# Order of wide and narrow matmuls inside a unit of the two-half blocks

## The chip, the cores and the metric

The kernel runs on one core of one Trainium2 chip. The metric is the device time of one execution in microseconds (us). The notes below use the names of the profile: PE is the matrix engine (TensorE), PEld its weight loads, DVE the vector engine, ACT the scalar engine, POOL GpSimd, and SP the engine that issues the weight stream's DMAs.

## The reference

Two transformer-like blocks for one sequence of 256 tokens of width 2048, all in float32. What matters here is that nearly all of the time goes into products of 256 tokens with large weight matrices:

```
def reference(x, ...):
    x = first_block(x, ...)       # h @ w_in, sliding-window attention, short conv, @ w_out, @ w_ple_gate
    return second_block(x, ...)   # @ w_in_2, recurrence, selected attention, @ w_o, then peer()

def peer(x, wq, keys1, keys2, u, v):      # 16384 experts, top 16 per head
    q = (xf @ wq) ...
    ...
    z = jnp.einsum('cd,ced->ce', xc, u[ec])
    act = jax.nn.gelu(z, approximate=False) * gc
    return jnp.einsum('ce,ced->cd', act, v[ec])
```

The kernel computes the expert layer densely: all of u and v (128 blocks of 128 experts each) is streamed and multiplied, and a table of gates picks the experts.

## The kernel before, in words

**Precision by halves.** Every float32 operand is split into a high part and a low part, and a product is made of three: high weights by high activations, high weights by low activations, and low weights by high activations.

**Units.** All weights arrive as one stream of 902 units of 128 x 1024 float32 (512 KB), in four slots of `raw`. For each unit ACT makes the high weights (`split_hi`, L495: `w_hi <- raw`, raises `hi_ready`) and DVE the low ones (`split_lo`, L504: `w_lo <- raw - w_hi`, raises `lo_ready`). PE multiplies, and its last matmul of a unit raises `unit_done`; ACT and DVE wait for `unit_done` of the unit four back before they write the same slot again. SP loads the next unit into a slot as soon as `lo_ready` shows that its `raw` was used. Every wait is written out by hand; there is no scheduler.

**Blocks of two-half form.** `halves_out` makes one block of 128 output columns from two units (`u` is 0 or 1), 8 slices of 128 rows of weights in each. For a slice, one *wide* matmul multiplies the high weights by high and low activations side by side (512 columns, L561, into all of a PSUM bank: low sums land in the upper half), and one *narrow* matmul multiplies the low weights by the high activations (256 columns, L568, added to the lower half). Behind the block ACT copies the upper half out (L574) and DVE adds the lower half to it (L579). 240 blocks, so 480 units, have this form: the stages conv, rnn, heads, wqu, u_decode, u_gates and u_late. Each stage is a loop on PE that calls `halves_out` and stands beside loops on ACT, DVE and POOL of the same stage.

**Two options.** `between` is called in a block's second unit only; in u_gates it is `two_tokens` (L2658), two small matmuls that build the table of gates from `hot` and `weighted`, which DVE writes. `paced` is set for one block, the first of wqu: there each wide matmul first waits for its slice of the activations (`act_lo_ready`, DVE L1959).

**The other forms.** In the last stage, `v` (L2693 to L2695), and in `tokens_out` (L601 to L603) the weights are the 512-column moving operand; all their matmuls are wide. These do not pass through `halves_out`.

Of the kernel before, what the change touches and what calls it, by code (L numbers as in the profile page):

```python
# [35 lines left out]
P = 128  # L36
S = 256
TT = S // P
D = 2048
KT = D // P  # L40
# [99 lines left out]
def build(nc, stream, x, p_t, rows, consts, params, rg_w, ukv, keys_t, out):  # L140
    ctx = ExitStack()
    with ctx:
        def sb(name, shape, dt=F32):
            return ctx.enter_context(nc.sbuf_tensor(name, shape, dt))

        def sem(name):
            return ctx.enter_context(nc.semaphore(name))
# [3 lines left out]
        w_hi = sb("w_hi", [P, SLOTS, UNIT], F32R)  # L151
        w_lo = sb("w_lo", [P, SLOTS, UNIT], F32R)
        act2 = sb("act2", [P, KT, 2, S], F32R)
        act_hi = act2[:, :, 0, :]
# [187 lines left out]
        lo_ready = sem("lo_ready")  # L342
# [29 lines left out]
        act_lo_ready = sem("act_lo_ready")  # L372
# [112 lines left out]
        def unit_slot(odd, u):  # L485
            return 2 * odd + u
# [65 lines left out]
        def halves_out(pe, pair, odd, bank, units=(0, 1), between=None, paced=None):  # L552

            for u in units:
                s = unit_slot(odd, u)
                pe.wait_ge(hi_ready, 2 * pair + u + 1)
                for kk in range(8):
                    k = 8 * u + kk
                    if paced:
                        pe.wait_ge(act_lo_ready, paced + k + 1)  # L560
                    pe.matmul(bank[:, :], w_hi[:, s, kk * P:(kk + 1) * P],  # L561
                              act2[:, k, :, :].rearrange("p a n -> p (a n)"), start=(k == 0), stop=False)
                if u and between:
                    between()
                pe.wait_ge(lo_ready, 2 * pair + u + 1)
                for kk in range(8):
                    k = 8 * u + kk
                    mm = pe.matmul(bank[:, 0:S], w_lo[:, s, kk * P:(kk + 1) * P], act_hi[:, k, :], start=False,  # L568
                                   stop=(k == KT - 1))
                mm.then_inc(unit_done, 1)  # L570

        def low_half(act, dest, bank):
# [1662 lines left out]
        def _(pe):  # L2235
# [89 lines left out]
            def conv_pair(j, n):  # L2325
                wait_summed(pe, block_of("conv", j, 4, n - 4))
                halves_out(pe, pair_of("conv", j, 4, n), odd_of("conv", n), banks[n])
# [141 lines left out]
            def rnn_inputs(j):  # L2469
                wait_summed(pe, block_of("rnn", j, 2, 0 - 2))  # L2470
                halves_out(pe, pair_of("rnn", j, 2, 0), odd_of("rnn", 0), banks[0])

            def rnn_queries(j):
                wait_summed(pe, block_of("rnn", j, 2, 1 - 2))
                halves_out(pe, pair_of("rnn", j, 2, 1), odd_of("rnn", 1), banks[1])
# [368 lines left out]
```

## Time and profile before

| what | value |
|---|---|
| median of 3 runs | 2696.33 us (2696.3 to 2696.57) |
| profiled execution, whole | 2696.89 us |
| its span, first to last instruction | 2695.2 us |
| PE busy | 2669.4 us (99% of the span) |
| granted TensorE clock, mean | 0.999 of full speed |
| matmuls in the span | 14299, of them 3840 wide and 3840 narrow in `halves_out` |

The span is what the trace shows; the profiled execution's own time is 1.69 us more, which lies around the span. Busy time of PE counts a matmul from its start until its modelled end, and consecutive matmuls overlap, so the rows that tell the pace of PE are the distances from one start to the next.

### The profile page before, as it was taken

The page shows a single profiled execution, that of the slowest core. Times are in us where ns is not written, and L with a number is a line of the kernel's source. Part 1 is how long each engine was busy: PE and PEld are TensorE (multiplying, and loading weights), DVE is VectorE, ACT ScalarE, POOL GpSimd, SP SyncE. Part 2 cuts the span into 40 slices and gives each one's busy share as a digit, 9 for nine tenths or more (in the row PEclk, how much of TensorE's full clock was granted, in tenths as well). Part 3 has the DMA queues.
Part 4 walks back from the last instruction along what each step waited for, and adds up shares of the span by engine and source line. Part 5 has one row for each costly group of instructions (what it writes and reads, how often), then busy time and mean ns, then how long its engine had stood idle before and what let it go on. Part 6 is the DMA issues. An engine that isn't in the chain of part 4 may idle for free.

```text
span 2695.2 us, 47112 instructions
## 1 busy us (share of the span) xinstructions
PE 2669.4 (99%) x14299; PEld 2298.4 (85%) x14299; DVE 1835.3 (68%) x2985; ACT 1369.4 (51%) x2066; POOL 371.4 (14%) x296
## 2 busy tenths in 40 slices
PE   8999999999999999999999999999999999999998
PEld 6888888898888998888888888888888888888887
DVE  6666665668987677489996777775565555555555
ACT  6454445555665444455455555554444444444444
POOL 0010000001011211011105555551000000000000
PEclk9999999999999999999999999999999999999999
DMA  7566555564554554655567777777976666666564
GB/s 257 189 216 213 181 199 177 177 219 159 172 176 156 167 168 157 195 201 186 195 201 212 202 202 203 201 204 218 305 240 217 217 217 219 212 220 216 200 241 156
DMA packets 204475, 543.26 MB, mean 202 GB/s; under 512 B 37504, under 2 KB 82816, under 8 KB 203392
## 3 DMA queue, kind: packets, MB, share of 16 engines
q1 hardware_dynamic: 148112, 486.74, 54.9%
q10 hardware_dynamic: 35568, 47.33, 5.0%
q0 software_dynamic: 20736, 8.46, 2.7%
q8 instruction: 30, 0.49, 0.1%
q14 instruction: 29, 0.24, 0.0%
HBM read 515.12 MB, written 27.33 MB: 201 GB/s over the span
## 4 chain that ended last, share of the span: by engine, by line
PE 94%; DVE 3%; ACT 1%; issue 1%; DMA 0%; SPq 0%; DVEq 0%; POOL 0%; ACTq 0%; POOLq 0%
PE bank L561 32%; PE bank L568 16%; PE bank L2693 8%; PE bank L2694 8%; PE bank L2695 8%; PE bank L601 4%; PE bank L603 4%; PE bank L602 4%; PE bank L2488 1%; DVE w_lo L504 1%; PE bank L527 1%; PE bank L528 1%; PE bank L529 1%; PE bank L2658 1%; PE bank L2465 0%
## 5 line engine op out<-in xcount | busy, mean ns | idle before, releaser
L504 DVE TENSOR_TENSOR w_lo<-raw,w_hi 128x1024 fp32r<-128x1024 f32 x902 | 1097.9, 1226 | 725.9 <-ACT w_hi L495 719.4
L495 ACT ACTIVATE w_hi<-raw 128x1024 fp32r<-128x1024 f32 x902 | 950.8, 1059 | 946.5 <-PE bank L568 363.1
L561 PE MATMUL bank<-act,w_hi 128*128 128x512 f32 x3840 | 975.2, 396 | 2.6 <-DVE cst L579 1.0
L561 PEld LDWEIGHTS bank<-act,w_hi 128*128 128x128 f32 x3840 | 692.0, 189 | 133.8 <-issue 6.4
L568 PEld LDWEIGHTS bank<-act,w_lo 128*128 128x128 f32 x3840 | 519.7, 190 | 33.1
L568 PE MATMUL bank<-act,w_lo 128*128 128x256 f32 x3840 | 535.6, 282 | 0.0
L2693 PE MATMUL bank<-w_hi,expert_act 128*128 128x512 f32 x1008 | 392.3, 389 | 0.1
L2694 PE MATMUL bank<-w_lo,expert_act 128*128 128x512 f32 x1008 | 392.2, 389 | 0.0
L2695 PE MATMUL bank<-w_hi,expert_act 128*128 128x512 f32 x1008 | 392.1, 389 | 0.0
L742 POOL DMA_INDIRECT g_kept<-slot_t x128 | 239.7, 1872 | 253.8 <-issue 170.4
L2693 PEld LDWEIGHTS bank<-w_hi,expert_act 128*128 128x128 f32 x1008 | 189.3, 188 | 39.6 <-DVE cst L579 0.5
L2695 PEld LDWEIGHTS bank<-w_hi,expert_act 128*128 128x128 f32 x1008 | 189.3, 188 | 39.3
L2694 PEld LDWEIGHTS bank<-w_lo,expert_act 128*128 128x128 f32 x1008 | 189.3, 188 | 39.1
L601 PE MATMUL bank<-w_hi,act 128*128 128x512 f32 x320 | 125.8, 393 | 2.0 <-DVE act L1401 1.1
L603 PE MATMUL bank<-w_hi,act 128*128 128x512 f32 x320 | 124.7, 390 | 0.0
L602 PE MATMUL bank<-w_lo,act 128*128 128x512 f32 x320 | 124.6, 389 | 0.0
L748 POOL TENSOR_TENSOR big<-big 128x1024 f32<-128x1024 f32 x2 | 5.8, 2878 | 839.4 <-DVE big L2196 839.4
L601 PEld LDWEIGHTS bank<-w_hi,act 128*128 128x128 f32 x320 | 60.1, 188 | 16.2 <-DVE w_lo L504 1.3
L603 PEld LDWEIGHTS bank<-w_hi,act 128*128 128x128 f32 x320 | 60.1, 188 | 12.6
L602 PEld LDWEIGHTS bank<-w_lo,act 128*128 128x128 f32 x320 | 60.1, 188 | 12.1
L729 POOL TENSOR_TENSOR big<-big 128x256 f32<-128x256 f32 x32 | 33.1, 1034 | 248.3 <-ACT big L1138 248.3
L2107 DVE SCALAR_TENSOR_TENSOR weighted<-cst,slot_t 128x256 fp32r<-128x256 f32 x128 | 61.3, 479 | 0.0
(344 smaller groups left out, 2498.4 us busy)
## 6 DMA issues: line engine op xcount, KB each, us to landing
raw<-in_stream SPq DMA_DIRECT2D x902, 512.0 KB
z_kept<-cst ACTq DMA_DIRECT2D x112, 128.0 KB, 2.4
cst<-z_kept ACTq DMA_DIRECT2D x112, 128.0 KB, 3.9
g_kept<-zeros POOLq DMA_DIRECT2D x16, 512.0 KB
big<-in_ukv ACTq DMA_DIRECT2D x16, 512.0 KB, 4.6
big<-g_kept SPq DMA_DIRECT2D x16, 512.0 KB, 5.6
big<-in_rows ACTq DMA_DIRECT2D x3, 1024.0 KB, 5.8
big<-in_x SPq DMA_DIRECT2D x2, 1024.0 KB, 10.2
```

The source lines that it names most:

```text
L495: act.activation(w_hi[:, s, :], raw[:, s, :], ACT.Copy).then_inc(hi_ready, 1)
L504: dve.tensor_tensor(w_lo[:, s, :], raw[:, s, :], w_hi[:, s, :].bitcast(F32), ALU.subtract).then_inc(lo_ready, 1)
L561: pe.matmul(bank[:, :], w_hi[:, s, kk * P:(kk + 1) * P], act2[:, k, :, :].rearrange("p a n -> p (a n)"), start=(k == 0), stop=False)
L568: mm = pe.matmul(bank[:, 0:S], w_lo[:, s, kk * P:(kk + 1) * P], act_hi[:, k, :], start=False, stop=(k == KT - 1))
L601: pe.matmul(outs[t], a_hi, hi, start=(k == 0), stop=False)
L602: pe.matmul(outs[t], a_hi, lo, start=False, stop=False)
L603: mm = pe.matmul(outs[t], a_lo, hi, start=False, stop=(k == KT - 1))
L742: pool.indirect_dma_start(g_kept, bass.IndirectOffsetOnAxis(ap=SLOT_INDEX[:, i:i + 1], axis=0), SLOT_GATE[:, i:i + 1], None, compute_op=AL ...
L2107: dve.scalar_tensor_tensor(out=weighted[:, tile, :, :], in0=iota.unsqueeze(1).broadcast_to([P, 2, P]), scalar=first_index[:, bass.ds(tok, 1)],
L2693: pe.matmul(o, a_hi, hi, start=first, stop=False, skip_group_check=True)
L2694: pe.matmul(o, a_hi, lo, start=False, stop=False, skip_group_check=True)
L2695: mm = pe.matmul(o, a_lo, hi, start=False, stop=False, skip_group_check=True)
```

## The change

In each unit the eight wide and eight narrow matmuls are issued in another order. Before: all eight wide ones, then `between` (second unit only), then the wait for the low weights, then all eight narrow ones. Now: four wide ones, then `between`, then the wait for the low weights, then the other four wide ones alternating with the first four narrow ones, then the last four narrow ones. The operands of each matmul, the bank it adds to, the number of instructions and the last matmul of the unit, which raises `unit_done`, are the same.

```diff
             for u in units:
                 s = unit_slot(odd, u)
                 pe.wait_ge(hi_ready, 2 * pair + u + 1)
-                for kk in range(8):
-                    k = 8 * u + kk
-                    if paced:
-                        pe.wait_ge(act_lo_ready, paced + k + 1)
-                    pe.matmul(bank[:, :], w_hi[:, s, kk * P:(kk + 1) * P],
-                              act2[:, k, :, :].rearrange("p a n -> p (a n)"), start=(k == 0), stop=False)
-                if u and between:
-                    between()
-                pe.wait_ge(lo_ready, 2 * pair + u + 1)
-                for kk in range(8):
-                    k = 8 * u + kk
-                    mm = pe.matmul(bank[:, 0:S], w_lo[:, s, kk * P:(kk + 1) * P], act_hi[:, k, :], start=False,
-                                   stop=(k == KT - 1))
+                for kk in range(12):
+                    if kk == 4:
+                        if u and between:
+                            between()
+                        pe.wait_ge(lo_ready, 2 * pair + u + 1)
+                    if kk < 8:
+                        k = 8 * u + kk
+                        if paced:
+                            pe.wait_ge(act_lo_ready, paced + k + 1)
+                        pe.matmul(bank[:, :], w_hi[:, s, kk * P:(kk + 1) * P],
+                                  act2[:, k, :, :].rearrange("p a n -> p (a n)"), start=(k == 0), stop=False)
+                    if kk >= 4:
+                        k = 8 * u + kk - 4
+                        mm = pe.matmul(bank[:, 0:S], w_lo[:, s, (kk - 4) * P:(kk - 3) * P], act_hi[:, k, :],
+                                       start=False, stop=(k == KT - 1))
                 mm.then_inc(unit_done, 1)
```

On PE, in the loop of stage u_late, one unit stood like this before (a row is an instruction or a run of equal ones, with the semaphores it waits for; L561 is the wide matmul, L568 the narrow one):

```order
L561 MATMUL bank<-act,w_hi 128x512 [waits hi_ready]
L561 MATMUL bank<-act,w_hi 128x512 x7
L568 MATMUL bank<-act,w_lo 128x256 [waits lo_ready]
L568 MATMUL bank<-act,w_lo 128x256 x7
```

The same unit now, where the wide matmul is L566 and the narrow one L570:

```order
L566 MATMUL bank<-act,w_hi 128x512 [waits hi_ready]
L566 MATMUL bank<-act,w_hi 128x512 x3
L566 MATMUL bank<-act,w_hi 128x512 [waits lo_ready]
L570 MATMUL bank<-act,w_lo 128x256
L566 MATMUL bank<-act,w_hi 128x512
L570 MATMUL bank<-act,w_lo 128x256
L566 MATMUL bank<-act,w_hi 128x512
L570 MATMUL bank<-act,w_lo 128x256
L566 MATMUL bank<-act,w_hi 128x512
L570 MATMUL bank<-act,w_lo 128x256 x5
```

Three narrow matmuls now stand between two wide ones, and the wait for the low weights has moved ahead of the fifth wide one.

On PE, in the second unit of a u_gates block, where the two token matmuls (L2658 before, L2660 now) stand, before:

```order
L561 MATMUL bank<-act,w_hi 128x512 [waits hi_ready]
L561 MATMUL bank<-act,w_hi 128x512 x7
L2655 REGISTER_ALU
L2656 ISA [waits gate_kept0]
L2658 MATMUL bank<-weighted,hot 128x256 [waits hot1]
L2658 MATMUL bank<-weighted,hot 128x256
L568 MATMUL bank<-act,w_lo 128x256 [waits lo_ready]
L568 MATMUL bank<-act,w_lo 128x256 x7
```

and now:

```order
L566 MATMUL bank<-act,w_hi 128x512 x3
L2657 REGISTER_ALU
L2658 ISA [waits gate_kept0]
L2660 MATMUL bank<-weighted,hot 128x256 [waits hot1]
L2660 MATMUL bank<-weighted,hot 128x256
L566 MATMUL bank<-act,w_hi 128x512 [waits lo_ready]
L570 MATMUL bank<-act,w_lo 128x256
L566 MATMUL bank<-act,w_hi 128x512
```

The token matmuls and their waits for `gate_kept` and `hot1` have moved ahead of four wide matmuls as well.

## Rows read from the trace of the kernel before

**Rows 1.** The page: busy time by engine, then the chain that ended last by engine and line.

```profile
PE 2669.4 (99%) x14299; PEld 2298.4 (85%) x14299; DVE 1835.3 (68%) x2985; ACT 1369.4 (51%) x2066; POOL 371.4 (14%) x296
...
PE 94%; DVE 3%; ACT 1%; issue 1%; DMA 0%; SPq 0%; DVEq 0%; POOL 0%; ACTq 0%; POOLq 0%
PE bank L561 32%; PE bank L568 16%; PE bank L2693 8%; PE bank L2694 8%; PE bank L2695 8%; PE bank L601 4%; PE bank L603 4%; PE bank L602 4%; PE bank L2488 1%; DVE w_lo L504 1%; PE bank L527 1%; PE bank L528 1%; PE bank L529 1%; PE bank L2658 1%; PE bank L2465 0%
```

**Rows 2.** The page's costliest groups: xcount | busy us, mean ns | idle before, by releaser.

```profile
L561 PE MATMUL bank<-act,w_hi 128*128 128x512 f32 x3840 | 975.2, 396 | 2.6 <-DVE cst L579 1.0
...
L568 PE MATMUL bank<-act,w_lo 128*128 128x256 f32 x3840 | 535.6, 282 | 0.0
```

**Rows 3.** The chain in order of time, stage u_late: start us, length us, what.

```profile
1934.88 1.84 PE bank L561 x8
1936.72 0.95 PE bank L568 x8
1937.67 1.84 PE bank L561 x8
```

**Rows 4.** The chain in order of time, stage u_gates, around two token matmuls.

```profile
1501.97 0.23 PE bank L2658 x2
1502.20 0.96 PE bank L568 x8
```

**Rows 5.** Timeline of PE, one unit of u_late and the next's first: start us, us.

```profile
1937.51 0.40 PE L561 MATMUL bank<-act,w_hi 128*128 128x512 f32 x1
...
1937.74 0.40 PE L561 MATMUL bank<-act,w_hi 128*128 128x512 f32 x1
...
1937.98 0.39 PE L561 MATMUL bank<-act,w_hi 128*128 128x512 f32 x1
...
1938.67 0.39 PE L561 MATMUL bank<-act,w_hi 128*128 128x512 f32 x1
...
1939.35 0.28 PE L568 MATMUL bank<-act,w_lo 128*128 128x256 f32 x1
...
1939.46 0.40 PE L568 MATMUL bank<-act,w_lo 128*128 128x256 f32 x2
...
1939.58 0.40 PE L568 MATMUL bank<-act,w_lo 128*128 128x256 f32 x2
...
1940.30 0.40 PE L561 MATMUL bank<-act,w_hi 128*128 128x512 f32 x1
```

**Rows 6.** Line L2693 of stage v: count, ns min/median/max, first and last start us.

```profile
L2693 PE MATMUL bank<-w_hi,expert_act x1008: 389/389/500, 1990.6 to 2675.7; 128*128 128x512 f32 x168
```

**Rows 7.** Timeline, stage rnn, around a late low half: start us, us, what.

```profile
622.25 3.05 DVE L504 TENSOR_TENSOR w_lo<-raw,w_hi 128x1024 fp32r<-128x1024 f32 x1
...
626.31 2.00 PE L561 MATMUL bank<-act,w_hi 128*128 128x512 f32 x8
...
628.15 1.12 PE L568 MATMUL bank<-act,w_lo 128*128 128x256 f32 x8
```

**Rows 8.** Timeline, stage u_gates, ahead of two token matmuls.

```profile
1806.17 0.48 DVE L2107 SCALAR_TENSOR_TENSOR weighted<-cst,slot_t 128x256 fp32r<-128x256 f32 x1
...
1808.78 2.00 PE L561 MATMUL bank<-act,w_hi 128*128 128x512 f32 x8
...
1810.62 0.40 PE L2658 MATMUL bank<-weighted,hot 128*128 128x256 f32 x2
```

**Rows 9.** Timeline of the paced block's second unit, PE and DVE.

```profile
1161.64 3.22 DVE L1959 SCALAR_TENSOR_TENSOR act<-bank,par,act 128x256 fp32r<-128x256 f32 x8
...
1162.26 3.15 PE L561 MATMUL bank<-act,w_hi 128*128 128x512 f32 x8 [0.17 <-DVE act L1959]
1165.24 1.00 PE L568 MATMUL bank<-act,w_lo 128*128 128x256 f32 x7
```

## The prediction

> **What bounds the kernel now.** I read the page first: PE is busy for 99% of the span, and the chain of work that ended last runs over PE for 94%, the wide and the narrow matmuls of `halves_out` alone for 32% and 16% [rows 1]. So the kernel is as long as PE's row of matmuls, and only two things can change it here: the distance from one matmul's start to the next, and waits of PE. Next the costliest groups: 3840 wide and 3840 narrow matmuls, that is 480 units of eight and eight, and idle time before them of 2.6 us and 0.0 us in all [rows 2]. No narrow matmul has waited for its low weights, so no wait is there to be removed. What is left is the pace.
>
> **The pace, read off the starts.** In order of time the chain shows a unit as 1.84 us of wide matmuls and 0.95 us of narrow ones, 2.79 us in all [rows 3]. The timeline of one unit tells more [rows 5]. The first five wide matmuls take 1938.67 - 1937.51 = 1.16 us, 0.232 each. The last three take 1939.35 - 1938.67 = 0.68 us, 0.227 each. That is the pace of stage v as well, where all matmuls are wide: (2675.7 - 1990.6) us over 1007 x 3 starts is 0.2268 us [rows 6]. Of the narrow ones the first takes 0.11 us, the second 0.12, and the other six 1940.30 - 1939.58 = 0.72 us, 0.120 each. The hundredths of a timeline are too coarse for the first, so I take it from the chain: eight narrow ones take 0.95 us behind a wide matmul [rows 3], and 0.96 us, eight times 0.120, behind the two token matmuls, which are narrow too and take 0.23 us together where two at 0.120 would take 0.24 [rows 4]. The first narrow matmul behind a wide one thus takes about 0.113 us, half of 0.227, and those behind another narrow one 0.119 to 0.120.
>
> So a switch has two sides. Going from wide to narrow, one matmul comes 0.007 us early. Going from narrow to wide, the wide ones are 0.005 us late on the mean, over five of them. A unit has one switch of each kind before and four of each now.
>
> **The change part by part.**
>
> Instructions: none is added or removed, and none of other engines moves; PE issues no DMA, and `unit_done` still stands on the last narrow matmul, so that ACT's and DVE's next units and SP's loads behind them follow a unit's end as before.
>
> Narrow matmuls: the first four now each stand behind a wide one. The second to fourth of them lose 0.119, 0.120 and 0.120 for 0.113: 0.020 us for a unit. The fifth then takes the second's place (0.119 for 0.120). That is 480 x 0.020 = 9.6 us, if each behaves as the first does now.
>
> Wide matmuls: the sixth to eighth now each stand behind a narrow one, where they were in the settled 0.227. The trace of before has no wide matmul behind a single narrow one. The bound from below is 0.227, no loss. The nearest row is the unit's first wide one, behind eight narrow ones: 0.23 us, and the second takes 0.24 [rows 5]. With the mean of 0.232 of the first five the three lose 3 x 0.005 = 0.015 us; with 0.007, what the narrow one had gained, 0.021; with the 0.236 that 0.24 may round from, 3 x 0.009 = 0.027. I take 0.020, equal to the gain: the nearest row by kind is the first wide one, and a 0.007 that a narrow one gets by having its weights ready, and that the wide one behind it then pays because its own weights had only the short narrow one to load under, is one and the same time. The sum of both terms is 0 for a unit.
>
> This is also where a rule speaks against the change. The Trainium skill (TensorE: Matmul & The Clock Gate, Step-by-step: what each phase is for) says that only the weight loads are pulled ahead, the next tile's weights loading while this tile's matmul runs, and that the matmuls keep their order. By it each narrow matmul has one load to cover, whatever stands behind it, and the eight of a unit cost the same in any order: a change of 0. No row of before shows a second load ahead, nor rules it out.
>
> The wait for the low weights moves up by four wide matmuls, 4 x 0.23 = 0.92 us. Queued behind it are those four and all narrow ones, and for them wait ACT and DVE (the slot) and the block's copy. The closest call that I found over the 480 units is in stage rnn, where a low half took 3.05 us and was done at 625.30; the narrow matmuls that need it began at 628.15, and the new place is 626.31 + 0.93 = 627.24 [rows 7]. So 1.9 us of cover remain where it is least, and the cost is 0. Were the cover gone, a unit would pay up to 0.92 us.
>
> The token matmuls move up as far. Their `weighted` was written by 1806.65 for a start at 1810.62 [rows 8]; of 3.97 us, 3.05 remain. Cost 0. They are a pair of narrow ones between wide ones now, a further switch in 64 units (two blocks in each of 32 turns): +0.007 for the wide one behind and as much less for the narrow one that they stood ahead of.
>
> The paced block: its second unit's wide matmuls come at the pace of DVE, 0.40 us each, 2.98 us from the first to the first narrow one [rows 9]. Three narrow ones of 0.12 now fit into three gaps of about 0.16: 0.36 us less, once.
>
> Sum: 0 - 0.4 us. The profiled execution took 2696.89 us (span 2695.2 and 1.69 around it), so 2696.5; the median of the runs stands 0.56 below the profiled one, which makes **2696.0 us**.
>
> **The rivals.**
>
> *Narrow ones hidden (faster).* The 0.120 of a narrow matmul behind a narrow one is a shortage (of weight loading or of issue, the row does not say which) that a wide one beside it makes good, and the wide one pays nothing. For it: the first narrow one does gain. Against it: eight wide ones in a row buy only about one narrow one its gain, and the next wide ones are late. Time: 480 x 0.020 = 9.6 us and the 0.4, so 2686.3. The Trainium skill (TensorE: Matmul & The Clock Gate, Wait — 56ns, not 53.3ns?) has a rule of this kind: without hardware decode the sequencer spends about 62 ns on a matmul; an estimate of two instructions by it gives 0.124 us for load and matmul, where the rows show 0.120, and by it the alternation would gain the 9.6 us.
>
> *Each switch is paid for (slower).* A wide matmul behind a narrow one starts the settling of five wide ones anew, and the narrow ones between do not get their 0.007 since the wide one ahead is not settled either. Place: the sixth to eighth wide matmul of each unit. Price: 0.005 to 0.009 each, 0.015 to 0.027 a unit, and 0.007 more if the first narrow one loses its gain too: 7 to 16 us, so 2703 to 2712, in the middle 2706. It decides from the point at which a pair of wide and narrow takes more than 0.347 (0.227 + 0.120) on the mean. For it: before, a unit is about 0.02 us longer than eight pairs of 0.347 (2.774 against 2.79), so a switch is not free in sum.
>
> *A wait takes its place.* The low weights are late at the new place. Against it the 1.9 us of cover; six units late by the whole 0.92 us would make 0.2%. I give it 2 in 100.
>
> **How the numbers follow.** About 0.2%, 5.4 us, or 0.011 us a unit, is what a measurement of this kernel can tell from no change. No change, 2696.0: 0.52. Narrow ones hidden: 0.22, nearly all beyond the limit. Switches paid for, the late low weights included: 0.26. The range reaches over the faster case's 2686.3 and takes the slower one's lower and middle part, to 2708; what lies above needs the highest price for all three wide ones. The likeliest case's own range is 2691 to 2701. Faster by over 0.2%: 0.22; within: 0.52; slower: 0.26.
>
> **What would show it.** In the changed trace a pair of wide and narrow in the alternation takes 0.347 us (0.340: hidden; 0.350 or more: paid for). Narrow starts in it come 0.113 apart from the next wide, and the wide ones there take 0.234. A unit of u_late stays at 2.79 us. Idle time before the wide and narrow groups stays under 3 us in all, and the wide ones of the paced block keep DVE's pace with narrow ones between them. The forecast is wrong if units differ by more than 0.011 us, or if PE waits for DVE's low half anywhere in `halves_out`.

## The result, and the profile after

The changed kernel takes 2701.26 us (median of 22 runs) where the kernel before takes 2696.39 us (22 runs): a ratio of 1.0018, 95% interval 1.0012 to 1.0024. It is slower by 4.9 us, less than the 0.2% that the prediction named as its limit, but clear of the noise of so many runs. (One of the 22 runs before took 4458.5 us; without it the median is 2696.35.) The forecast was 2696.0 with no change as the likeliest; the time lies in the whole range, on the slower side, and 0.3 us above the 2701 at which the range of no change ended.

The page of the changed kernel, to be held against [rows 1, 2]: busy time by engine, the chain that ended last, the two groups of matmuls, which now have the lines L566 (wide) and L570 (narrow).

```profile
span 2699.4 us, 47114 instructions
...
PE 2674.1 (99%) x14299; PEld 2296.5 (85%) x14299; DVE 1835.0 (68%) x2985; ACT 1370.1 (51%) x2066; POOL 370.9 (14%) x296
...
PE 93%; DVE 4%; ACT 1%; issue 1%; DMA 0%; SPq 0%; POOL 0%; DVEq 0%; ACTq 0%; POOLq 0%
...
L566 PE MATMUL bank<-act,w_hi 128*128 128x512 f32 x3840 | 1162.9, 398 | 2.4 <-DVE big L1508 0.8
...
L570 PE MATMUL bank<-act,w_lo 128*128 128x256 f32 x3840 | 766.2, 281 | 0.0
```

PE is as full as before, and nothing stands idle ahead of the wide and narrow matmuls: 2.4 and 0.0 us. The busy sums of the groups (1162.9 and 766.2 us, before 975.2 and 535.6) tell nothing of cost: consecutive records overlap, and when the two lines alternate the overlap is counted in both. The span is 4.2 us longer. None of it is idle time ahead of these two groups, so it lies in the pace of PE or in waits of other matmuls; below, both turn up.

The timeline of PE, one unit of u_late, to be held against [rows 5]:

```profile
1941.30 1.32 PE L566 MATMUL bank<-act,w_hi 128*128 128x512 f32 x5
1942.46 0.28 PE L570 MATMUL bank<-act,w_lo 128*128 128x256 f32 x1
1942.58 0.40 PE L566 MATMUL bank<-act,w_hi 128*128 128x512 f32 x1
1942.81 0.28 PE L570 MATMUL bank<-act,w_lo 128*128 128x256 f32 x1
1942.93 0.40 PE L566 MATMUL bank<-act,w_hi 128*128 128x512 f32 x1
1943.17 0.28 PE L570 MATMUL bank<-act,w_lo 128*128 128x256 f32 x1
1943.29 0.40 PE L566 MATMUL bank<-act,w_hi 128*128 128x512 f32 x1
1943.52 0.76 PE L570 MATMUL bank<-act,w_lo 128*128 128x256 f32 x5
1944.12 1.32 PE L566 MATMUL bank<-act,w_hi 128*128 128x512 f32 x5
```

The unit takes 1944.12 - 1941.30 = 2.82 us, before 2.79. The three wide matmuls that stand behind a narrow one take 0.23, 0.24 and 0.23 us. The trace keeps starts to the nanosecond; the distances from each start to the next, as medians over the units of u_late, are (W wide, n narrow):

```
before  W 233 236 228 232 231 227 227 227   n 113 119 120 120 120 120 120 120            unit 2793 ns
after   W 233 236 228 233 231  n 113 W 233 n 117 W 241 n 120 W 236 n 113   n 119 120 120 120   unit 2813 ns
```

The eight wide ones take 30 ns more (6, 14 and 9 in the three that moved), the narrow ones 10 ns less. 20 ns in 32 units is 0.64 us, and that is what u_late has grown by, from 89.27 to 89.91 us between its first wide and its last narrow start. By the same measure conv grew by 0.40 us, rnn by 0.96, heads by 0.09, wqu by 0.77, u_decode by 0.11 and u_gates by 1.57. That is 4.5 us in all; the rest of the kernel took some 0.3 us less.

Of the 1.57 us in u_gates a part is a wait. The waits of PE have one row that the kernel before did not have, and the timeline shows its place, the first token pair of the stage:

```profile
PE bank L2660 <- DVE weighted L2109: 0.8, 1, 0.8
```

```profile
1443.52 1.09 PE L566 MATMUL bank<-act,w_hi 128*128 128x512 f32 x4
1445.40 0.50 PE L2660 MATMUL bank<-weighted,hot 128*128 128x256 f32 x2 [0.78 <-DVE weighted L2109]
```

The block's first unit began at 1440.71 and the next block at 1447.62 us, 6.91 us; before it was 5.98 (1438.75 to 1444.73). So 0.93 us are lost there, once.

In the other 63 token units the alternation runs at another pace. The timeline of one in u_gates:

```profile
1502.88 1.09 PE L566 MATMUL bank<-act,w_hi 128*128 128x512 f32 x4
1503.81 0.40 PE L2660 MATMUL bank<-weighted,hot 128*128 128x256 f32 x2
1504.04 0.39 PE L566 MATMUL bank<-act,w_hi 128*128 128x512 f32 x1
1504.27 0.28 PE L570 MATMUL bank<-act,w_lo 128*128 128x256 f32 x1
1504.39 0.39 PE L566 MATMUL bank<-act,w_hi 128*128 128x512 f32 x1
...
1505.08 0.39 PE L566 MATMUL bank<-act,w_hi 128*128 128x512 f32 x1
1505.31 0.75 PE L570 MATMUL bank<-act,w_lo 128*128 128x256 f32 x5
```

From 1504.04 to 1505.08 three pairs of a wide and a narrow matmul take 1.04 us, where the three pairs of the u_late unit from 1942.46 to 1943.52 take 1.06. The same instructions on the same shapes take 0.347 us a pair here and 0.353 there. Over the whole kernel the three pairs ran at the fast pace in 120 units (63 in u_gates, 26 in conv, 22 in heads, 5 in u_decode, 4 in rnn) and at the slow pace in the other 360, but for one that keeps DVE's pace (the second unit of the paced block). From its first to its last start a fast unit takes 7 ns less than the same unit before, 0.87 us in all. A slow one takes 16 ns more on the mean, 5.6 us in all (the unit that waits for the tokens and the two units of the paced block are left out of this).

### The profile page after: what moved, and what is told of

The parts are those of the page before. It is cut to its first block, busy times and chain, and to the rows that moved or that the text cites. A ratio compares the mean times of both kernels' runs of the same rounds, so it can differ in the third digit from the quotient of the medians.

```text
span 2699.4 us, 47114 instructions
## 1 busy us (share of the span) xinstructions
PE 2674.1 (99%) x14299; PEld 2296.5 (85%) x14299; DVE 1835.0 (68%) x2985; ACT 1370.1 (51%) x2066; POOL 370.9 (14%) x296
## 4 chain that ended last, share of the span: by engine, by line
PE 93%; DVE 4%; ACT 1%; issue 1%; DMA 0%; SPq 0%; POOL 0%; DVEq 0%; ACTq 0%; POOLq 0%
PE bank L566 31%; PE bank L570 16%; PE bank L2695 8%; PE bank L2696 8%; PE bank L2697 8%; PE bank L603 4%; PE bank L605 4%; PE bank L604 4%; DVE w_lo L504 1%; PE bank L2490 1%; PE bank L527 1%; PE bank L528 1%; PE bank L529 1%; PE bank L2660 1%; ACT w_hi L495 1%
## 5 line engine op out<-in xcount | busy, mean ns | idle before, releaser
L566 PE MATMUL bank<-act,w_hi 128*128 128x512 f32 x3840 | 1162.9, 398 | 2.4 <-DVE big L1508 0.8
L566 PEld LDWEIGHTS bank<-act,w_hi 128*128 128x128 f32 x3840 | 691.5, 189 | 133.2 <-issue 6.3
L570 PE MATMUL bank<-act,w_lo 128*128 128x256 f32 x3840 | 766.2, 281 | 0.0
L570 PEld LDWEIGHTS bank<-act,w_lo 128*128 128x128 f32 x3840 | 622.7, 189 | 39.9
```

Source lines behind the costliest of these rows:

```text
L566: pe.matmul(bank[:, :], w_hi[:, s, kk * P:(kk + 1) * P], act2[:, k, :, :].rearrange("p a n -> p (a n)"), start=(k == 0), stop=False)
L570: mm = pe.matmul(bank[:, 0:S], w_lo[:, s, (kk - 4) * P:(kk - 3) * P], act_hi[:, k, :], start=False, stop=(k == KT - 1))
```

## The experiments

The order in a unit is given by a string: W is the next wide matmul, n the next narrow one. Experiments 1, 2, 6, 7 and 10 keep the instructions of a unit and change their order alone; 3 and 4 widen the narrow matmuls, 5 gives the two units of a block different orders, 8 uses another bank and 9 adds matmuls. Each cut shows only the lines that matter, and `...` stands for what is left out. The names ORDER, BETWEEN_AT (the place of the token matmuls) and WAIT_AT (the place of the wait for the low weights) stand for values that each kernel has written in.

```diff
-                for kk in range(12):
+                wide = narrow = 0
+                for at, form in enumerate(ORDER):
+                    if at == BETWEEN_AT and u and between:
+                        between()
+                    if at == WAIT_AT:
+                        pe.wait_ge(lo_ready, 2 * pair + u + 1)
...
```

**1. The early wait and tokens without the alternation.** "Alternation" is the stretch in which wide and narrow matmuls take turns.

```diff
+ORDER = "WWWWWWWWnnnnnnnn"; BETWEEN_AT = WAIT_AT = 4
```

> The order of the matmuls of before (eight wide, eight narrow); only the wait for the low weights and the two token matmuls stand behind the fourth wide one, as in the change. Theory A (the alternation itself costs, in the pace of the matmuls): no difference from before beyond 2 us, a unit of u_late stays at 2.79 us, no idle time ahead of a wide or narrow matmul beyond 3 us in all. Rival B (the early wait or the early token matmuls cost): 4 to 5 us slower than before, 2701.

Measured: 2698.0 us, ratio 1.0006 (0.9997 to 1.0016). The units of u_late take 2.793 us as before: the wait itself costs nothing. In u_gates alone the stage grew by 1.76 us (462.33 to 464.09): the first token pair waits here too (6.91 us for that block, 0.93 more than before), and the others are a switch more in the run of wide matmuls. The chain in order of time shows it: four wide ones ahead of the pair, four behind, and those take 0.93 us, where four settled ones take 0.91.

```profile
1506.38 0.93 PE bank L567 x4
1507.31 0.23 PE bank L2663 x2
1507.54 0.93 PE bank L567 x4
1508.47 0.96 PE bank L572 x8
```

So neither theory was right as put: outside u_gates no stage grew by more than 0.05 us, so there it is the alternation that costs, as theory A said, but in u_gates the early place of the tokens costs too. The time as a whole cannot be told from before.

**2. Full alternation.**

```diff
+ORDER = "WnWnWnWnWnWnWnWn"; BETWEEN_AT = 4; WAIT_AT = 1
```

> All eight pairs alternate (wide, narrow, wide, ...), with the low weights waited for behind the first wide one. Theory A1 (each switch from narrow to wide is paid for, 4.9 us for three further ones): seven further ones cost 7/3 as much, 11 us slower, 2708, a pair takes 0.350 us on the mean. Rival A2 (the pace depends on how the matmuls stand to each other when the alternation begins; in a steady alternation they fall into the pairs of 0.230 and 0.117 that the token units of the change show): a unit of u_late takes 8 x 0.347 = 2.78 us instead of 2.79, some 8 us faster than before, 2688.

Measured: 2705.1 us, ratio 1.0032 (1.0019 to 1.0045): 8.6 us slower, between the two forecasts and with the sign of A1. A2's time was a miss, but the trace bears out its view that the pace depends on how the alternation is entered: steady stretches run at one of two paces. Timeline of PE, first in u_decode, then in u_late:

```profile
1365.93 0.39 PE L567 MATMUL bank<-act,w_hi 128*128 128x512 f32 x1
1366.16 0.28 PE L572 MATMUL bank<-act,w_lo 128*128 128x256 f32 x1
1366.28 0.39 PE L567 MATMUL bank<-act,w_hi 128*128 128x512 f32 x1
...
1368.01 0.39 PE L567 MATMUL bank<-act,w_hi 128*128 128x512 f32 x1
```

```profile
1949.97 0.40 PE L567 MATMUL bank<-act,w_hi 128*128 128x512 f32 x1
1950.21 0.28 PE L572 MATMUL bank<-act,w_lo 128*128 128x256 f32 x1
1950.33 0.40 PE L567 MATMUL bank<-act,w_hi 128*128 128x512 f32 x1
...
1952.09 0.40 PE L567 MATMUL bank<-act,w_hi 128*128 128x512 f32 x1
```

Six pairs take 2.08 us in the first (0.347 each) and 2.12 us in the second (0.353). To the nanosecond the first repeats 230 117, elsewhere 231 112 233 117, both with a mean of 0.347 us a pair; the second repeats every three pairs 233 117 241 120 236 113, which is what the units of the change run through. Within u_decode the pace turns from the first to the second ahead of the stage's last turn, where three small transposes of PE stand between the units:

```
unit of u_decode   starts at us   distances of its 16 starts, each to the next, ns
28                 1424.99        230 117 230 116 230 117 230 117 230 116 230 117 230 117 230 118
29                 1428.01        315 117 233 118 241 120 236 113 232 118 241 120 236 113 232 118
30                 1430.92        241 120 236 113 232 118 241 120 236 113 232 118 241 120 236 113
```

All of u_gates and u_late then stays at the second (u_gates is 6.4 us longer than before, u_late 1.1); conv, heads and wqu, which PE's other work cuts into short stretches, show both, and are no slower than before (201.39, 254.21 and 186.99 us against 201.45, 254.25 and 187.67). In rnn, cut up as well, 62 of 64 units ran at the second, and it is 1.6 us longer.

**3 and 4. Narrow matmuls of 384 columns,** in the order of before and in that of the change. The low weights then also multiply a part of the low activations, a small product more.

```diff
-                    mm = pe.matmul(bank[:, 0:S], w_lo[...], act_hi[:, k, :], ...)
+                    mm = pe.matmul(bank[:, 0:384], w_lo[...], act2[:, k, :, :].rearrange("p a n -> p (a n)")[:, 0:384], ...)
```

> The order of before, but the narrow matmuls are 384 columns wide (the low weights also multiply the low activations of half the tokens, which adds a small product to the upper sums). Theory L (a 256-column matmul is too short to cover the next weight load, and a wide one behind it pays): at 384 columns there is no shortage, narrow ones come at 384/512 of 0.2267, 0.170 us, all wide ones at 0.227, a unit of u_late takes 3.17 us. Rival F (a switch of form or a fixed cost of each matmul, whatever the load): 0.173 us for a narrow one (0.120 plus 128 columns at 0.107 per 256) and the first five wide ones still at 0.232: 3.22 us. Time some 480 x 0.38 = 180 us above before, 2878.

> The order of the change with narrow matmuls of 384 columns, to be compared with the kernel of 384 columns in the order of before. Theory L (short cover of the weight load): no difference between the two, within 2 us. Rival F (each switch of form costs): again 4 to 5 us slower than that kernel.

Measured: 2913.4 and 2913.8 us, the same within their spread; the forecast of 2878 was 35 us too low. The chain of the first, with wide matmuls at 1.85 us for eight and narrow ones at 1.42, 0.177 each:

```profile
1944.85 1.39 PE bank L572 x8
1946.24 1.85 PE bank L567 x8
1948.09 1.42 PE bank L572 x8
```

A unit of u_late takes 3.267 us in the order of before and 3.260 alternating. Both are above theory L's 3.17 and rival F's 3.22. The narrow ones reach 0.173, rival F's number, in the last two of eight, and the wide ones behind them do not settle at all within eight (229 233 236 224 231 236 228 233 ns). So theory L, that a narrow matmul of 256 columns is too short to cover the next weight load, falls by experiment 3: at 384 columns the wide ones behind are even less settled. Its forecast for experiment 4, no difference, came true, but not for its reason: an alternating pair takes 0.407 to 0.411 us in u_late, where a settled wide and a settled narrow one would take 0.400, so the alternation is off the settled pace here too, and the runs of eight that it replaces are about as far off. Rival F falls in its second half: the switches of the change add nothing to the time there.

**5. Mirrored units.** The second unit of a block runs its narrow matmuls first.

```diff
+                order = "nnnnnnnnWWWWWWWW" if u and not paced else "WWWWWWWWnnnnnnnn"
```

> The first unit of a block as before (eight wide, eight narrow); the second the other way round (eight narrow, then eight wide), so that the narrow matmuls of a block stand in one run of sixteen and the wide ones of two blocks too: half the switches of before. The paced block keeps the old order. Every theory by which a switch from narrow to wide costs about 0.020 us more than a switch back gives (0.027 over five wide ones against 0.007) says 240 x 0.020 = 4.9 us faster: 2691.6, two units of u_late take 5.566 us instead of 5.587. If what counts is only the state in which a stretch is entered and the wide ones behind sixteen narrow ones settle more slowly or not at all, it is no faster: 2696 or above.

Measured: 2695.0 us, ratio 0.9997 (0.9988 to 1.0006): no difference that can be told. Two units of u_late take 2.766 + 2.801 = 5.567 us, where 5.566 was expected, and the chain shows the runs of sixteen:

```profile
1940.37 1.91 PE bank L574 x16
1942.28 3.65 PE bank L568 x16
1945.93 1.91 PE bank L574 x16
```

But u_gates, from its first start to u_late's, took 461.75 us where it took 462.45 before: it gained 0.7 us instead of 80 x 0.020 = 1.6. The forecast of 2691.6 was a miss: the span fell by 2.1 us, not 4.9. Sums for a stage made from one unit's pace held in u_late and not in u_gates.

**6. Two narrow ones ahead of the alternation.**

```diff
+ORDER = "WWWWnnWnWnWnWnnn"; BETWEEN_AT = WAIT_AT = 4
```

> Order in a unit: four wide, two narrow, then the other four wide alternating with four narrow, then two narrow: one switch more than the change has. Theory P (an alternation runs in one of two repeating patterns, 0.347 us or 0.353 us for a pair, by the state in which it is entered; entered behind two narrow ones, as the token units of the change show, it runs in the fast one): the wide ones in it take 0.230, the narrow ones 0.117, a unit of u_late 2.78 to 2.79 us, 4 to 8 us faster than before, 2688 to 2692. Rival A1 (every further switch from narrow to wide is paid for alike, 1.6 us each over the kernel): four further ones, 6.5 us slower than before, 2703.

Measured: 2703.1 us, ratio 1.0025 (1.0015 to 1.0035). My forecast for theory P was a miss: in u_late the wide and narrow ones run through 233 118 240 120 236 114 232 118, the slow pattern, and a unit takes 2.820 us. In heads, where other matmuls stand between the units, the same order runs at the fast pace in 31 of 64 units. Two narrow matmuls ahead do not by themselves choose the pattern. The time is rival A1's 2703, and so is the unit: with one switch more than the change it takes 7 ns more.

**7. The tokens late, in the change.**

```diff
+ORDER = "WWWWWnWnWnWnnnnn"; BETWEEN_AT = 11; WAIT_AT = 4
```

> The change, but the two token matmuls stand behind the eighth wide matmul again instead of behind the fourth. Theory P (the token pair makes its unit's alternation start in the fast pattern): without it these 64 units run in the slow pattern like the others, and the change is 1 to 3 us slower than it was: 2702.5 to 2704, u_gates from its first wide to its last narrow matmul 465 to 467 us where the change took 463.9. Rival B (the early token pair is itself what costs there, 1.8 us in u_gates in the kernel that only moved it): faster than the change by that, 2699.5, u_gates 462.2.

Measured: 2702.6 us, ratio 1.0023 (1.0013 to 1.0032); u_gates 465.37 us. That is theory P: the first token pair no longer waits (5.87 us for that block), yet u_gates is 1.47 us longer than in the change, because the token units now run 113 233 117 241 120 236 as the others do. Only the trace can tell this: by the runs as a whole, the interval overlaps with that of the change (1.0012 to 1.0024). In u_gates the two parts of the change do not add up: before 462.33 us, with the early tokens alone 464.09 (experiment 1), with the alternation alone 465.37 (here), with both 463.90.

**8. The narrow matmuls in a bank of their own,** in u_late alone, in the order of the change.

```diff
+                        mm = pe.matmul((bank if other is None else other)[:, 0:S], w_lo[...], act_hi[:, k, :], ...)
...
+                    halves_out(pe, ..., banks[2 + n], other=banks[6 + n])
```

> The order of the change; in stage u_late alone the narrow matmuls add up in a PSUM bank of their own, which nothing reads (that stage's low-weight terms are left out of the sums). Theory Q (what costs is that a half-bank and a whole-bank matmul follow each other in one bank): in u_late the pattern 0.233, 0.117, 0.241, 0.120, 0.236, 0.113 is gone and a unit takes 2.79 us or less. Theory P (it is the state in which the alternation is entered, on the operands' side): the same pattern as in the change, 2.813 us a unit.

Measured, a single run: 2701.1 us; u_late 89.91 us, a unit 2.813, the same pattern. Theory Q falls. The order in u_gates is that of the change here, and again 63 of its 64 token units run at the fast pace.

**9. One matmul inserted ahead of each turn of u_late,** in the full alternation.

```diff
-            with pe.Fori(0, LATE // 2) as i:
+            for i in range(LATE // 2):
+                pe.matmul(banks[7][:, 0:64 * (i + 1)], act_hi[:, 0, 0:P],
+                          act2[:, 0, :, :].rearrange("p a n -> p (a n)")[:, 0:64 * (i + 1)], start=True, stop=True)
```

> All eight pairs alternate as in the full alternation; the eight turns of stage u_late are written out, and ahead of each stands one further matmul of 64, 128, ... 512 columns into a bank that nothing reads. Theory P (the state at the entry decides between 0.347 and 0.353 us a pair): u_late, which ran at 0.353 throughout, now shows both paces, one or the other for whole turns, changing where a matmul was inserted. Rival T (the stage decides: its operands, its transfers): 0.353 in all eight turns, but for the first few pairs behind the inserted matmul.

Measured, a single run: 2705.0 us. The timeline of PE around the second inserted matmul (L2677, 128 columns): six pairs ahead of it, from 1916.08 to 1918.20, and six behind it, from 1919.38 to 1921.46.

```profile
1916.08 0.40 PE L567 MATMUL bank<-act,w_hi 128*128 128x512 f32 x1
...
1918.20 0.40 PE L567 MATMUL bank<-act,w_hi 128*128 128x512 f32 x1
...
1918.91 0.22 PE L2677 MATMUL bank<-act 128*128 128x128 f32 x1
...
1919.38 0.40 PE L567 MATMUL bank<-act,w_hi 128*128 128x512 f32 x1
...
1921.46 0.40 PE L567 MATMUL bank<-act,w_hi 128*128 128x512 f32 x1
```

2.12 us before, 2.08 us behind. Turn by turn u_late ran slow (64 columns), fast (128), slow (192), slow (256), and fast in the last four (320 to 512), each pace held to the end of its turn. That is theory P's forecast; rival T falls, since all eight turns belong to the same stage.

The same trace shows that the order of the instructions is not the whole of the entry. Up to u_late this kernel gives PE the instructions of experiment 2 in the same order. Yet u_decode runs at the fast pace in 28 of 32 units there and in 2 of 32 here. They ran on different chips; whether that, or a wait on the way to u_decode, made the difference is not known. So a stage's pace can differ from one execution to another, and there is one trace of each kernel.

**10. One pair alone.**

```diff
+ORDER = "WWWWWWWnWnnnnnnn"; BETWEEN_AT = WAIT_AT = 7
```

> Seven wide matmuls, one narrow, the eighth wide, seven narrow: one further switch of each kind, where the change has three. Theory A1 (each switch costs alike): a third of the change's 0.020 us, 2.800 us for a unit of u_late, 1.6 us slower in all. Theory P (the slow pattern's first pair is no longer than 0.347, its second and third are): 2.797 us or less for a unit, 0 to 1.9 us slower in all.

Measured, a single run: 2698.9 us; a unit of u_late takes 2.800 us, A1's number and not P's. Its wide one behind the first narrow one takes 232 and the narrow one next 118, about as P has it, but the narrow ones that follow do not settle at 120 either (121 120 124 117 118 121), and the next unit begins with 237 235. What P leaves out is that a run of narrow matmuls can be entered unsettled as well.

## Why the prediction was wrong, point by point

**The bound and the cover: right.** PE's pace is what the time follows. The wait for the low weights at its new place cost nothing (0.0 us idle ahead of L570; experiment 1's unit of u_late). The paced block's two units took 6.99 us from the first wide one's start to the next block's, where they took 7.35 before: 0.35 us less, with 0.36 forecast.

**The narrow and the wide terms: mis-sized, both to the slow side.** The step that failed is "the sum of both terms is 0 for a unit". I let every narrow matmul behind a wide one gain 0.007 us as the first does in [rows 5], 0.020 in all, and let the wide ones lose as much. In u_late the narrow ones gained 0.010 and the wide ones lost 0.030, more than my upper bound of 0.027 from the second wide one of a unit. 0.020 us of the sum is left, in the units that run so. The picture of one and the same time passed from a narrow to a wide matmul was wrong: the pair does not keep a sum of 0.347 us. The prediction's own signs say the same: a unit of u_late differs by more than 0.011 us, and its pairs take more than 0.350. The time fell inside the range because the range took in part of the slower rival, not because the sum held.

**What stands in its place.** A steady alternation ran at one of two paces, 0.347 or 0.353 us for a pair, in repeating patterns, and how it is entered decides which. Experiment 9 shows it most directly: its eight turns differ only in the columns of the matmul inserted ahead of each, and whole turns run at one pace or the other. Experiment 2 shows the pace turning within one stage, behind three transposes, and 7 shows that the token pair is what put the token units of the change on the faster pace. In u_late the change enters the slow one, three pairs of it in a unit: 3 x 0.0067 = 0.020 us, which is the whole growth of the unit. Over the kernel 359 of 480 units enter the slow one, and in heads and conv, where a third or more enter the fast one, the stage grows less. What it is in PE that the entry sets is not shown.

**The token matmuls: wrong.** I read the cover of a pair late in the stage, 3.97 us [rows 8], and costed the move at 0. The first pair has no such cover: it waits 0.78 us, and its block is 0.93 us longer. Even before, that pair started 0.28 us behind the wide matmul ahead of it, where the settled distance is 0.227. The row to read was that of the stage's first turn. Beyond the wait, the pair between the wide ones cost some 0.8 us over the other 63 units in experiment 1, and with the alternation it brought the faster pace instead; the prediction had put this switch at nothing in sum.

**The rivals.** Hidden narrow ones fell: eight switches of each kind instead of one cost 8.6 us rather than gain (experiment 2). The rule of the Trainium skill beside that rival (TensorE: Matmul & The Clock Gate, Wait — 56ns, not 53.3ns?) would, by the estimate made from it, have given a gain as well, and the trace does not show one. The other rule of the Trainium skill (TensorE: Matmul & The Clock Gate, Step-by-step: what each phase is for), that the weights of the next tile load while this tile's matmul runs, agrees with the traces: in u_late each weight load starts 1 to 5 ns behind the start of the matmul ahead of its own, before the change and after it. So no second load ran ahead, which the prediction had left open. The conclusion that I drew from that rule, the same cost in any order, does not hold: the order and what ran before make a difference. The slower rival named the right place, the sixth to eighth wide matmul, with a price per unit of 0.015 to 0.027 us against 0.020 measured in u_late. Its time, 2706 in the middle, was too high because not all units pay: u_late does in full, 120 units in other stages do not. Its picture, a settling that each switch starts anew, does not hold either: seven further switches should then cost 7/3 of three, 47 ns a unit in u_late, and cost 34 (experiment 2). What a switch costs in u_late is the slow pace of its pair: one, three and four further switches cost 7, 20 and 27 ns a unit (experiment 10, the change, experiment 6), 6.7 each. In full alternation eight slow pairs cost 53 ns, but the settling of a run of wide ones, 20 ns net of the quick first narrow one, no longer arises, which leaves 34. At the fast pace a switch costs nothing: a unit of the last turns of experiment 9 takes 2.77 us, less than the 2.793 before. Late low weights, the third rival, did not occur.

**What stays open.** Why PE has two paces, and why a plain run of wide matmuls takes five to settle at 0.227, is not explained. Too few columns in the narrow matmul to cover a load (3), one bank for both forms (8) and the stage by itself (9) are ruled out as the sole cause; 8, 9 and 10 rest on a single run each. Whether the patterns come from how the moving operand and the weights are read against each other was not tried. Two narrow matmuls ahead did not bring the fast pace in u_late (6), while the two token matmuls of the same width did in u_gates; why is not known. No version here beats the kernel before beyond its noise (5).

## What to carry to other kernels

On a kernel that is bound by back-to-back matmuls, the distances between starts are the profile to read, position by position, and a change of order must be priced from rows with the same neighbours on both sides; where no such row exists, one trial run is worth more than a bound by the nearest one. Before moving an instruction up, read its cover in the first turn of the loop, not in the middle. Regrouping that leaves the instructions the same moved the time here by at most 9 us in 2696, and not in proportion to the number of switches. Sums made from one stage did not hold in the others.

## What was not expected of the hardware

- Full alternation of 512- and 256-column matmuls ran at two paces, 2.08 and 2.12 us for six pairs, under the same granted clock (0.999 over the run); one extra matmul (of 128, 192 or 320 columns in experiment 9), or three transposes, turned one into the other, and each then held, the slow one through all 192 units of u_gates and u_late in experiment 2, past its 64 token pairs.
- A matmul settled in a run of its kind takes 226.7 or 120.0 ns for 512 or 256 columns; of 384 columns, the last two in a run of eight take 173.3 (experiment 3). The three fit 53.3 ns for each 128 columns and 13.3 ns on top for each matmul. The first narrow one of 256 columns behind settled wide ones takes 113.
- Behind a run of narrow matmuls of 256 columns the first five wide ones take some 27 ns more than settled ones, 233 236 228 232 231 ns, the same to 1 or 2 ns in conv, u_decode, u_gates and u_late.
